# PEER feed-forward: expert tables streamed once and multiplied densely, in place of gathered rows

## The reference, cut to what matters

```python
def peer_ffn(h, w_query, sub_keys, expert_u, expert_v):      # per block of 128 tokens
    q = (xt @ w_query).reshape(TOKEN_BLOCK, PEER_HEADS, 2, PEER_HALF)
    s = jnp.einsum('thpd,hpnd->thpn', q, sub_keys)            # two lists of 128 scores
    s_top, i_top = lax.top_k(s, K)                            # K = 16, PEER_HEADS = 8
    cand = (s_top[:, :, 0, :, None] + s_top[:, :, 1, None, :]).reshape(TOKEN_BLOCK, PEER_HEADS, K * K)
    cand_idx = (i_top[:, :, 0, :, None] * N_KEYS + i_top[:, :, 1, None, :]).reshape(...)
    best, pos = lax.top_k(cand, K)
    idx = jnp.take_along_axis(cand_idx, pos, axis=-1)         # 16 experts for each token and head
    g = jax.nn.softmax(best, axis=-1)
    u = expert_u[idx]
    v = expert_v[idx]
    act = jax.nn.gelu(jnp.einsum('td,thkd->thk', xt, u))
    return jnp.einsum('thk,thkd->td', (g * act).astype(xt.dtype), v)
```

## Time and profile before

| | us |
|---|---|
| median of 3 runs (1661.51 to 1664.16) | 1662.12 |
| time of the profiled execution | 1663.22 |
| its span | 1661.4 |
| PE, DVE, ACT and POOL busy in the span | 1471.6, 877.0, 473.9, 291.6 |
| mean granted TensorE clock | 0.957 |

### The profile page before, as it was taken

The page is one execution under the profiler, slowest core; times in us unless marked ns, Lnnn a source line. Parts: engine busy times, 40 slices in busy tenths (PEclk is TensorE's granted clock), DMA queues, the critical chain, the costliest instruction groups (busy, mean ns, idle before and its releaser), DMA issues.

```text
span 1661.4 us, 24559 instructions
## 1 busy us (share of the span) xinstructions
PE 1471.6 (89%) x9594; PEld 1173.7 (71%) x9594; DVE 877.0 (53%) x2235; ACT 473.9 (29%) x1258; POOL 291.6 (18%) x260
## 2 busy tenths in 40 slices
PE   2999999898888888898888899999999888888888
PEld 1888887798888888888788747888755544445445
DVE  5787756977777777777775546521342111111112
ACT  1152212444444444444443312210211111111111
POOL 0000000354445444444444100000000000000000
PEclk7999999999999999999999999999999998999999
DMA  9554786799999999999999986566579999999996
GB/s 390 230 203 152 296 336 259 325 420 421 420 418 413 419 416 421 420 416 420 419 415 421 369 329 255 202 264 252 194 313 391 429 430 432 429 430 434 430 432 279
DMA packets 57112, 595.76 MB, mean 359 GB/s; under 512 B 6464, under 2 KB 6848, under 8 KB 8000
## 3 DMA queue, kind: packets, MB, share of 16 engines
q1 hardware_dynamic: 20160, 326.12, 47.5%
q0 software_dynamic: 36864, 268.45, 39.0%
HBM read 593.50 MB, written 1.05 MB: 358 GB/s over the span
## 4 chain that ended last, share of the span: by engine, by line
PE 54%; DMA 32%; DVE 10%; issue 2%; ACT 1%; SPq 0%; POOL 0%; DVEq 0%; POOLq 0%
PE bank L644 20%; DMA weight_slabs<-in_w_moe 17%; PE bank L865 15%; DMA gathered_rows<-in_expert_uv,work 10%; PE bank L988 5%; DMA weight_slabs<-in_expert_uv,work 3%; PE bank L891 3%; PE bank L800 2%; PE bank L965 2%; DVE weight_slabs L1696 1%; DVE gathered_rows L1696 1%; PE bank L663 1%; DVE weight_slabs L1349 1%; PE bank L1016 1%; DMA columns<-in_columns 1%
## 5 line engine op out<-in xcount | busy, mean ns | idle before, releaser
L865 PE MATMUL bank<-work,weight_slabs 128*128 128x128 f32 x2048 | 271.7, 295 | 68.4 <-ACT work L1212 68.3
L865 PEld LDWEIGHTS bank<-work,weight_slabs 128*128 128x128 f32 x2048 | 264.3, 209 | 79.6 <-ACT work L1212 77.1
L865 PE MATMUL bank<-work,gathered_rows 128*128 128x128 f32 x2048 | 250.1, 278 | 20.9 <-ACT work L1212 20.9
L865 PEld LDWEIGHTS bank<-work,gathered_rows 128*128 128x128 f32 x2048 | 241.4, 193 | 31.8 <-ACT work L1212 29.2
L1696 DVE CUSTOM_DVE_ANT_0 gathered_rows<-gathered_rows,work 128x1024 f32<-128x1024 f32 x128 | 156.8, 1227 | 141.5 <-DMA gathered_rows<-in_expert_uv,work 141.5
L644 PE MATMUL bank<-hT,weight_slabs 128*128 128x256 f32 x992 | 219.8, 382 | 0.7 <-ACT hT L1069 0.7
L1285 POOL DMA_INDIRECT gathered_rows<-in_expert_uv,work x128 | 143.3, 1120 | 437.4 <-DVE work L1667 297.9
L644 PEld LDWEIGHTS bank<-hT,weight_slabs 128*128 128x128 f32 x992 | 188.6, 191 | 30.5 <-issue 2.8
L1285 POOL DMA_INDIRECT weight_slabs<-in_expert_uv,work x128 | 148.1, 1157 | 203.9 <-PE bank L865 199.6
L988 PE MATMUL bank<-weight_slabs,work 128*32 128x512 f32 x992 | 130.5, 673 | 48.8 <-DMA weight_slabs<-in_w_moe 47.6
L1696 DVE CUSTOM_DVE_ANT_0 weight_slabs<-weight_slabs,work 128x1024 f32<-128x1024 f32 x128 | 151.6, 1222 | 37.0 <-DMA weight_slabs<-in_expert_uv,work 36.9
(11 more groups left out here) (329 smaller groups left out, 1613.5 us busy)
## 6 DMA issues: line engine op xcount, KB each, us to landing
weight_slabs<-in_w_moe SPq DMA_DIRECT2D x29, 4096.0 KB, 23.8
weight_slabs<-in_slabs SPq DMA_DIRECT2D x55, 2048.0 KB, 12.1
weight_slabs<-in_w_moe SPq DMA_DIRECT2D x35, 2048.0 KB, 20.1
gathered_rows<-in_w_moe SPq DMA_DIRECT2D x2, 2048.0 KB, 14.6
weight_slabs<-in_slabs SPq DMA_DIRECT2D x2, 1024.0 KB, 10.5
gathered_rows<-in_expert_uv,work POOLq DMA_INDIRECT x128, 13.3
weight_slabs<-in_expert_uv,work POOLq DMA_INDIRECT x128, 12.0
weight_slabs<-in_slabs SPq DMA_DIRECT2D x1, 1664.0 KB, 28.4
```

The costliest lines, as they stand in the source:

```text
L865: last = nc.tensor.matmul(ps[c // 2][:, (c % 2) * T + t * P:(c % 2) * T + (t + 1) * P], row_at[k][:, D + c * P:D + (c + 1) * P], diag[:, k ...
```

## The change

Every token picks experts of its own, but together 256 tokens pick 32768 times from 16384 experts. The changed kernel doesn't gather. It reads both tables once, in 64 rounds of 256 experts each:

- **u rounds** (64): H = U x tokens for 256 experts and 256 tokens, 16 matmuls of 256 columns from a 1 MB piece of `u_stream`. ACT applies gelu from the bank into one of four `kept` buffers, and GpSimd writes the buffer to memory (`spill`, 256 KB), except those of the last four rounds.
- **gate matrix**: for each token, PE multiplies a 128 x 128 one-hot matrix of second keys (one row for each of its 128 picks) with a one-hot matrix of first keys scaled by the gates. The product is the token's 128 x 128 gate matrix. DVE builds both matrices (`hot_group`: 4 tokens, 8 instructions of 128x128), PE multiplies (`gate_group`), ACT copies the bank into `gates0` or `gates1`, which together fill all eight slots. The groups of token tile 0 stand in u rounds 17 to 24 and those of tile 1 in rounds 52 to 59, four in each. `turn_chosen` ahead of each set (`tr0`, `tr1`) transposes the chosen keys and gates.
- **v rounds** (64): GpSimd reads `kept` back, DVE multiplies it with the gates, PE multiplies a 1 MB piece of `v_stream` with it, 16 matmuls of 256 columns, into banks 0 to 3.

The loads of both streams are issued by SP in places of the slab order, ahead of `w_query0`, `w_query2`, `in2_0`, `in2_1`, `in2_2` and `bda4`. The small softmax and the routing stay as they were, but routing now runs for eight heads of tile 0, then its 32 hot groups, then eight heads of tile 1, then 32 hot groups. The parts of the diff below stand in the order PE, ACT, GpSimd, DVE, SP.

```diff
+        group = 0
+        for p in range(NROUND):
+            if p < PH:
+                query(p)
+            if p in first_rounds() or p in second_rounds():
+                u_round(p, group)
+                group += 4
+            else:
+                u_round(p)
+            if p < PH:
+                key_scores(p)
+            if p == FIRST_TILE - 1:
+                turn_chosen(0)
+            if p == SECOND_TILE - 1:
+                turn_chosen(1)
...
+        def gate_group(n):
+            b = begin(f"gb{n}")
+            pe.wait_ge(hot_ready, n + 1)
+            for q in range(4):
+                last = nc.tensor.matmul(b[:, q * P:(q + 1) * P], hot_rows[:, n % 2, q, 0, :], hot_rows[:, n % 2, q, 1, :],
...
+        def u_round(p, group=None):
+            w = stream_at[STREAM[p]].rearrange("p (a c n) -> p a c n", a=2, c=DC)
+            pe.wait_ge(stream_in[STREAM[p]], stream_value[p])
+            b = begin(f"u{p}")
+            for a in range(2):
+                for k in range(DC):
+                    last = nc.tensor.matmul(b[:, a * T:(a + 1) * T], w[:, a, k, :], hT[:, k, :], start=(k == 0), stop=(k == DC - 1))
...
+                    if group is not None and k % 4 == 3:
+                        gate_group(group + 2 * a + k // 4)
...
-        for m in range(NPAIR):
-            for r in range(TOPK):
-                n = m * TOPK + r
-                expert_row(m % 2, r % NROW, n + 1, closing=n == NPAIR * TOPK - 1)
...
+        for k in range(NROUND):
+            q = NROUND + k
+            w = stream_at[STREAM[q]].rearrange("p (a n) -> p a n", a=2)
+            pe.wait_ge(stream_in[STREAM[q]], stream_value[q])
+            pe.wait_ge(weighed, k + 1)
...
+                    last = nc.tensor.matmul(ps[c // 2][:, (c % 2) * T:(c % 2 + 1) * T], w[:, a, c * P:(c + 1) * P], kept[k % 4][:, a, :],
...
+        def hidden_out(p):
+            b = take(f"u{p}")[:, :].rearrange("p (a t) -> p a t", a=2)
+            if p >= 4:
+                act.wait_ge(kept_out[p % 4], 16 * (p // 4))
+            freed(A(kept[p % 4], b, ACT.Gelu_apprx_tanh))
...
+        for p in range(NROUND - 4):
+            wait_emptied(pool, f"u{p}")
+            nc.gpsimd.dma_start(spill[p + 4].rearrange("p (a t) -> p a t", a=2), kept[p % 4]).then_inc(kept_out[p % 4], 16)
+        for k in range(4, NROUND):
+            pool.wait_ge(kept_out[k % 4], 16 * (k // 4))
+            pool.wait_ge(v_done, k - 3)
+            nc.gpsimd.dma_start(kept[k % 4], spill[k].rearrange("p (a t) -> p a t", a=2)).then_inc(kept_in[k % 4], 16)
...
+        def hot_group(n):
+            if n >= 2:
+                dve.wait_ge(chunk_ready, INDEX[f"gb{n - 2}"] + 1)
+            for q in range(4):
+                c = (4 * n if n < 32 else second_token(n - 32)) + q
+                V.tensor_scalar(hot_rows[:, n % 2, q, 0, :], K("iota"), chosenT[:, 1, c:c + 1], None, ALU.is_equal)
+                ins = V.tensor_scalar(hot_rows[:, n % 2, q, 1, :], K("iota"), chosenT[:, 0, c:c + 1], chosenT[:, 2, c:c + 1],
+                                      ALU.is_equal, ALU.mult)
+            ins.then_inc(hot_ready, 1)
...
+        for k in range(NROUND):
...
+            V.tensor_tensor(kept[k % 4][:, :, 0:P], kept[k % 4][:, :, 0:P], gates0[:, 2 * k:2 * k + 2, :], ALU.mult)
+            V.tensor_tensor(kept[k % 4][:, :, P:T], kept[k % 4][:, :, P:T], gates1[:, :, 2 * k:2 * k + 2].rearrange("p t i -> p i t"), ALU.mult)\
+                .then_inc(weighed, 1)
...
-            if name == "in2_0":
-                for k in range(NROW):
-                    sp.wait_ge(row_in[k], 16 * NPAIR * TOPK // NROW)
-            if name in late[4:6]:
-                sp.wait_ge(chunk_ready, INDEX["acc3"] + 1)
+            if name in late[0:6]:
+                sp.wait_ge(weighed, 16 * min(late.index(name) + 1, 4))
```

More of the change, by code:

```diff
@@ L187, in second_fill, with first_rounds, second_rounds, second_token @@
     return fill
+def first_rounds():
+    return range(FIRST_TILE, FIRST_TILE + 8)
+def second_rounds():
+    return range(SECOND_TILE, SECOND_TILE + 8)
+def second_token(group):
+    return (32, 64, 0, 96)[group // 8] + 4 * (group % 8)
 def make_plan():
@@ L475, in program @@
[L475 to L483, removed]
+    hot_rows = view(6144, 2048, "p (b q s n) -> p b q s n", b=2, q=4, s=2)
@@ L568, in _ @@
             sp.dma_start(slot_view(SLOT[n])[:, 0:words], src).then_inc(slab_loaded[SLOT[n]], 16)
[L570 removed]
+        both = arena[:, 0:NSLOT * SLAB]
         def load_first(src, slot):
@@ L792, in _, with query @@
         sum_squares("ss2", 1)
-        def query(h, a=0, z=2 * DC):
+        def query(h):
             w = slab3(8, 512)(slab(f"w_query{h // 2}"))
[L796 to L802, removed]
+            b = begin(f"pq{h}")
+            for p in range(2):
+                for k in range(DC):
+                    if h == 0 and p == 0:
+                        pe.wait_ge(h_ready, DC + k + 1)
+                    f0 = T * (h % 2) + p * P
+                    last = nc.tensor.matmul(b[:, p * T:(p + 1) * T], w[:, k, f0:f0 + P], hT[:, k, :], start=(k == 0), stop=(k == DC - 1))
+            done(last)
         def key_scores(h):
@@ L814, in key_scores @@
             done(last)
[L816 to L831, removed]
+        def turn_chosen(t):
+            b = begin(f"tr{t}")
+            pe.wait_ge(chosen_ready, t + 1)
+            for a in range(3):
+                last = nc.tensor.transpose(b[:, a * P:(a + 1) * P], chosen[:, a, :], ident)
+            done(last)
+        def gate_group(n):
[3 more added lines that the diff above has]
+                last = nc.tensor.matmul(b[:, q * P:(q + 1) * P], hot_rows[:, n % 2, q, 0, :], hot_rows[:, n % 2, q, 1, :],
@@ L832, in first_scores @@
                                         start=True, stop=True)
             done(last)
[L835 to L854, removed]
-        pe.wait_ge(zero_ready, 1)
[L857 to L870, removed]
@@ new lines, in _ @@
+        group = 0
+        for p in range(NROUND):
+            if p < PH:
+                query_out(p)
+            if p in first_rounds() or p in second_rounds():
+                for i in range(3):
+                    gates_out(group + i)
+                hidden_out(p)
+                gates_out(group + 3)
+                group += 4
+            else:
+                hidden_out(p)
+            if p < PH:
+                scores_out(p)
+            if p == FIRST_TILE - 1:
+                soft(0)
+            if p == SECOND_TILE - 1:
+                soft(1)
@@ L1637, in route @@
+        def route(t, h):
+            then(V.tensor_copy(stage, sc[:, t, h, :]), plain=True)
             top16([(stop_[:, q, :], itop[:, q, :], stage[:, q * NKEY:(q + 1) * NKEY]) for q in range(2)])
@@ new lines, in route, with gates @@
+            then(ins)
+            then(V.tensor_reduce(out=chosen[:, 0:2, TOPK * h:TOPK * (h + 1)], in_=hot[:, :, :, :], axis=AX.X, op=ALU.add))
+        def gates(t):
+            dve.wait_ge(best_exp, t + 1)
+            g3 = chosen[:, 2, :].rearrange("p (h k) -> p h k", h=PH)
+            then(V.tensor_reduce(out=gsum[:, 0, :], in_=g3, axis=AX.X, op=ALU.add))
+            then(V.reciprocal(gsum[:, 1, :], gsum[:, 0, :]))
+            V.tensor_tensor(g3, g3, gsum[:, 1, :].unsqueeze(2).to_broadcast([P, PH, TOPK]), ALU.mult).then_inc(chosen_ready, 1)
+            freed(f"tr{t}", V.tensor_copy(chosenT[:, :, :], take(f"tr{t}")[:, 0:3 * P].rearrange("p (a n) -> p a n", a=3)))
```

371 lines of the change are left out of this document (181 added, 190 removed).

## The result

The changed kernel is slower: 2018.18 us in the median of 4 runs (2015.55 to 2019.36), beside 1662.57 (1661.51 to 1664.16) for the kernel before in the same session. The ratio is 1.214, with a 95% interval of 1.213 to 1.216. The prediction said 1548, range 1525 to 1603, and gave slower a chance of 0.04. It was wrong.

What follows compares the result with a forecast made beforehand. The prediction took PEER to be bound by the gathers' bytes. With them replaced by streams, PEER would end 117.5 us sooner: 1661.4 - 117.5 + 3 = 1546.9 span, + 1.8 = 1548.7, so 1548, range 1525 to 1603.

Steps and rivals of the forecast that it cites:

- TensorE: Matmul prices in PEER: 0.216 us for 256 columns, 0.111 for 128, so 3.46 us a u or v round.
- 1. to the end of round 16, from PEER's start: Start of PEER: eight queries, 17 u rounds, eight scores and a 1.7 us wait for `hT`, 91.7 us.
- 7. v rounds: Last stage of PEER: 64 v rounds of 3.46 us, 221.1 us, ending PEER at 834.2.
- collisions on the DMA engines: Allowance in the v rounds for stream and read-back meeting three slabs: 3 us added to the span.
- What bounds the kernel before: PEER of the kernel before was bound by the gathers' bytes: 268 MB, DMA 99% busy over 666.6 us.
- Hot groups: Gate matrices in rounds 17-24 and 52-59: VectorE sets the pace at 1.87 us a group, 59.8 a tile.
- Routing, exp and the stages behind PEER: Routing takes 9.9 us a pair, about 1.9 us follows exp, and everything behind PEER keeps its length.
- DMA and read-back hidden: Stream and read-back hide beside 3.46 us rounds; read-back of 7.1 to 10.4 us, under the 10.4 limit.
- read-back or full DMA: Rival: in the v rounds the read-back paces, 1592 us, or DMA at its upper bound, 1570; chance 0.15.
- GpSimd held up by VectorE: Rival: DMA issues wait for VectorE in hot rounds, 32 us in all, giving 1580; chance 0.09.
- Clock: After idle stretches at `tr0` and `tr1` a lower TensorE clock costs 2.5 us, hidden by VectorE; hot rounds 70% busy.
- The rival on the other side: Slower than before: read-back under load makes v rounds 5.36 us, needing an 18.0 us read-back; chance 0.03.

Runs made afterwards that it cites:

- before_half_mm: The kernel before the change, with four of each gather's eight matmuls left out; 1662.85 us.
- u_half_k: The changed kernel with every second feature chunk only in the u rounds, 8 matmuls instead of 16; 1803.18 us.
- half: The changed kernel with float16 operands for u, v and gate matmuls, streams cast by GpSimd's DMA queue, spill and read-back issued by ACT; 1511.71 us.
- no_stream: The changed kernel with each stream buffer filled once only and hidden values not read back; 2016.31 us.
- half_eight: The float16 kernel `half` with eight buffers for hidden values in place of four; 1512.22 us.
- half_v_less: The float16 kernel `half`, four buffers, with only one half of each v stream piece loaded; 1499.95 us.
- half_eight_v_less: The eight-buffer float16 kernel `half_eight` with only one half of each v stream piece loaded; 1441.48 us.

## Why the prediction was wrong, point by point

**The step that failed** is the first line of "TensorE": "A matmul with 256 moving columns costs 55.25/256 = 0.216 us in a dense stretch, one with 128 columns 1.78/16 = 0.111 us". The 256 and the 16 are records; the matmuls are 128 and 8, and the costs 0.432 and 0.22 us. Every term that rests on it doubled. By the prediction's own list, in us:

| step | forecast | measured |
|---|---|---|
| 1. to the end of round 16, from PEER's start | 91.7 | 181.8 (284.3 to 466.1) |
| 2. exp, softmax, transposes | 4.2 | 4.2 (to 470.3) |
| 3. hot groups of tile 0 | 60.3 | 85.0 (to 555.3) |
| 4. rounds 25 to 51 | 93.3 | 186.5 |
| 5. second gap and hot groups | 4.3 + 60.3 | 3.9 + 85.4 |
| 6. rounds 60 to 63 | 13.8 | 27.6 |
| 7. v rounds | 221.1 | 445.5 (to 1304.2) |

The v rounds' 445.5 us are 64 x 6.91 = 442.2 and 3.4 for four statements of 512 columns that clear the sum banks, which the forecast's list left out. The end of PEER was forecast at 834.2 and came at 1304.2, 470.0 later. The 3 us allowed for collisions on the DMA engines weren't needed. The other 1.4 us lie behind PEER (0.8) and outside the span (0.6). Together this is the miss of 2017.1 - 1548.7 = 468.4 us.

- *What bounds the kernel before*: right, shown by `before_half_mm`.
- *Hot groups*: VectorE's 1.87 us a group was nearly right as VectorE's own cost: in `u_half_k`, where VectorE was busy for 49.00 of 49 us (418 to 467), a group came every 1.82 us. Its two instructions follow each other after 0.20 and 0.26 us, as worked out from the earlier trace rows, and in `half` 32 groups took some 59 us. But which engine paces was wrong: TensorE needs 1.73 + 0.89 = 2.62 us for what stands beside a group, not 1.30. VectorE's timeline in the changed kernel shows it waiting, and for whom:

```profile
482.00 0.29 DVE L1729 TENSOR_SCALAR work<-constants_sb,work 128x128 f32<-128x128 f32 x1 [0.71 <-PE bank L895]
482.20 0.34 DVE L1730 TENSOR_SCALAR work<-constants_sb,work 128x128 f32<-128x128 f32 x1
```

- *Routing, exp and the stages behind PEER*: right. A pair takes 9.9 us. The second block's chain starts 353.5 us later than before (1305.7 against 952.2) and all of it keeps its length: the spans differ by 353.3.
- *DMA and read-back hidden*: right in this kernel, but not by the forecast's reasoning, as TensorE left twice the time (`no_stream`). At the forecast's own pace it is shown for u rounds only, by `u_half_k` with 3.45 us a round:

```profile
470.00:560.00 90.00, 90.00 (x422) 79.31 (x422) 74.06 (x366) 15.99 (x27) 14.03 (x26) 1.00 0.97 366
```

  TensorE has no gap there, with the DMA engines at 0.97. No run has v rounds of 3.46 us. At 1.75 us of TensorE, in `half`, full DMA engines pace them at 3.1 us, even with a read-back of half the size. So the rival "read-back or full DMA" was a real mechanism; whether it would have held at 3.46 us stays open.
- *GpSimd held up by VectorE*: not in this kernel, and not in `u_half_k`, where VectorE never rested in the hot rounds: GpSimd's issues of the spill took 0.54 us in the median and 0.68 at most. See below for `half_eight`.
- *Clock*: right, a granted clock of 0.99 over PEER and 0.98 in the hot rounds, where TensorE was 98% busy. The forecast had it 70% busy there, which didn't occur. In `half`, TensorE was busy for 36.76 of 58.5 us in the first set (388.5 to 447), and the granted clock was 0.71. It cost nothing that can be seen there, as VectorE paced. The 64 "matmuls" of the forecast's clock paragraph are records, 32 matmuls.
- *The rival on the other side* named the wrong mechanism. It asked that a v round reach 5.36 us by the read-back. The v rounds are 6.91 by TensorE alone, so the bound that it worked out was passed by a term that I had taken as known and given no bound at all.

The forecast that this change would have deserved from the same rows: 128 x 6.91 for the rounds, 8 x (6.91 + 0.89) for the heads, 64 x 0.89 for the gates is 1004 us of TensorE, against 666.6 us for the whole of PEER before. That sum decides alone.

## What to carry to other kernels

Before a chain's length is divided by its count, count the matmuls of that stretch in the code: the ratio of records to statements is part of the price, and here it was 2 for float32, 1 for float16 and 1 for transposes of float32. A trade of bytes for arithmetic is first a sum of dense float32 columns on TensorE; this one paid only where the operands were 16 bits wide. The price that carries every term needs a bound like the small ones do. And when a stage goes faster, look for the resource that it left idle before: here it went from full DMA engines to full TensorE and, at 16 bits, to VectorE in the hot rounds and back to full DMA engines in the v rounds.

## What the runs showed of the hardware

- In a dense stretch a float32 matmul of 256 columns takes 0.432 us and has two weight loads of 190 ns beneath it; a float16 one takes 0.109 us and has one load of 98 to 105 ns.
- A float32 matmul leaves two records in the trace, a float16 one and a float32 transpose one each.
- A DMA that casts float32 to float16 is counted by what it writes, but takes the engines' time by about what it reads: 246 GB/s shown with the engines full.
- GpSimd DMA issues lasted many times their usual length while VectorE was busy, and ended with its hot groups. In `half_eight`, with VectorE busy without a gap in the hot rounds (42.00 of 42 us from 397 to 439), GpSimd's timeline shows:

```profile
418.49 0.53 POOL L1347 DMA_DIRECT2D arena<-in_u_stream  x1 [5.82 <-PE bank L876]
425.73 16.39 POOL L1347 DMA_DIRECT2D arena<-in_u_stream  x3 [6.71 <-PE bank L876]
```

  One of these three issues took 15.3 us where the usual one takes 0.53. VectorE's last hot instruction began at 440.30 us, and the window from 426.2 to 441.0 has GpSimd busy throughout. `half_v_less` and `half_eight_v_less` have such an issue too (14.7 and 15.3 us), and all three have a second one at the end of the second set (7.2 to 7.9 us). Each ended 0.1 to 0.4 us after VectorE's last hot instruction, so VectorE is the likely cause, though no run was made to test it. `half` had VectorE as full in its hot rounds and no issue over 0.58 us there, and up to the v rounds it is the same program as `half_v_less`. So it doesn't happen in every execution; what decides isn't known. The Trainium skill ("SBUF — State Buffer", "SBUF: two separate sides") says that VectorE's two-port instructions lock GpSimd out of writing descriptors, which fits these three kernels and not `half`. It cost no time here that can be seen, as the v rounds behind it wait for bytes.
